# Gate products on tokens and remainders side by side in the dense feed-forwards of a two-block transformer kernel

## The reference

```python
def swiglu(h, w_gate, w_up, w_down):
    return (jax.nn.silu(h @ w_gate) * (h @ w_up)) @ w_down

# first block, layer i (0 and 1)
    h = rms_norm(x, ffn_norm[i]) * (1.0 + sc_f) + sh_f
    x = x + g_f * swiglu(h, ffn_w_gate[i], ffn_w_up[i], ffn_w_down[i])
# second block, layer 0
    h = layer_norm(alpha * h + g2 * swiglu_2(h * (1 + sc2) + sh2, ffn_gate, ffn_up, ffn_down), ln_g, ln_b)
```

## Time and profile before

| | us |
|---|---|
| median of 3 runs (lowest, highest) | 2221.87 (2220.83, 2222.57) |
| profiled execution | 2224.2 |
| its span | 2222.3 |
| TensorE busy | 2176.0 (98%) |
| VectorE busy | 1852.4 (83%) |
| ScalarE busy | 1335.8 (60%) |
| GpSimd busy | 86.2 (4%) |
| ada rows, issue to landing, median | 8.0 |

### The profile page before, as it was taken

How to read it: one execution, slowest core, us unless ns; L and a number is a source line. 1 busy time by engine, 2 the same in 40 slices (tenths; PEclk the granted TensorE clock), 3 DMA queues, 4 the chain that set the end, 5 groups by cost and what they waited for, 6 DMA issues and landing times.

```text
span 2222.3 us, 32055 instructions
## 1 busy us (share of the span) xinstructions
PE 2176.0 (98%) x13109; PEld 1918.6 (86%) x13123; DVE 1852.4 (83%) x2332; ACT 1335.8 (60%) x1508; POOL 86.2 (4%) x140
## 2 busy tenths in 40 slices
PE   6999999999999999999999999999999999999998
PEld 4888999889999979999798888888888888888886
DVE  7867888876998677888896988888888988888897
ACT  3574433665343776434633877777767777777775
POOL 3000111000010000010000000000000000000000
PEclk9999999999999999999999999999999999999999
DMA  9845988625887616885553999999999999999991
GB/s 369 297 186 200 341 325 300 227 77 209 303 298 272 223 39 253 307 332 187 204 201 105 369 348 369 344 370 351 353 366 345 364 346 369 344 364 354 357 363 70
DMA packets 259218, 633.33 MB, mean 285 GB/s; under 512 B 9304, under 2 KB 21625, under 8 KB 258554
## 3 DMA queue, kind: packets, MB, share of 16 engines
q1 hardware_dynamic: 234554, 536.83, 66.4%
q0 software_dynamic: 24512, 94.38, 11.4%
HBM read 630.13 MB, written 1.05 MB: 284 GB/s over the span
## 4 chain that ended last, share of the span: by engine, by line
PE 83%; DVE 11%; DMA 3%; issue 2%; ACT 1%; SPq 0%; POOL 0%; ACTq 0%; DVEq 0%
PE ps L1225 81%; DVE wring_rounded L3019 3%; DMA aring<-in_ada_rows 3%; DVE aring L3046 2%; DVE work L3019 1%; PE ps L2284 1%; PE ps L1421 1%; DVE OT L3043 1%; DVE F L3026 1%; DVE X L3026 0%; DVE F L3019 0%; PE ps L1396 0%; ACT scr_rounded L2349 0%; ACT F_rounded L2349 0%; DVE work_rounded L3019 0%
## 5 line engine op out<-in xcount | busy, mean ns | idle before, releaser
L3019 DVE TENSOR_TENSOR wring_rounded<-wring,scr_rounded 128x2048 fp32r<-128x2048 f32 (+1 forms) x314 | 568.9, 1840 | 76.0 <-ACT scr_rounded L2349 75.9
L2349 ACT ACTIVATE scr_rounded<-wring 128x2048 fp32r<-128x2048 f32 (+1 forms) x314 | 480.0, 1554 | 194.9 <-PE ps L1225 131.4
L1225 PE MATMUL ps<-wring_rounded,OT_rounded 128*128 128x512 f32 (+1 forms) x1184 | 314.8, 390 | 2.7 <-DVE wring_rounded L3019 1.7
L1225 PEld LDWEIGHTS ps<-wring_rounded,OT_rounded 128*128 128x128 f32 x1184 | 220.1, 188 | 47.2 <-DVE wring_rounded L3019 2.3
L3046 DVE CUSTOM_DVE_ANT_0 aring<-aring,F,vec 128x1024 f32<-128x1024 f32 x152 | 187.9, 1283 | 34.2 <-DMA aring<-in_ada_rows 33.5
L3019 DVE TENSOR_TENSOR wring_rounded<-wring,H_rounded 128x2048 fp32r<-128x2048 f32 (+1 forms) x85 | 193.3, 2275 | 25.5 <-ACT H_rounded L2349 25.3
L3019 DVE TENSOR_TENSOR wring_rounded<-wring,aring_rounded 128x2048 fp32r<-128x2048 f32 x84 | 192.4, 2290 | 16.2 <-ACT aring_rounded L2349 16.2
L2349 ACT ACTIVATE H_rounded<-wring 128x2048 fp32r<-128x2048 f32 (+1 forms) x85 | 162.4, 1910 | 61.0 <-issue 39.5
L2349 ACT ACTIVATE aring_rounded<-wring 128x2048 fp32r<-128x2048 f32 x84 | 161.2, 1919 | 58.1 <-PE ps L1225 57.4
L1225 PE MATMUL ps<-V_rounded,wring_rounded 128*128 128x256 f32 x1184 | 177.9, 285 | 4.6 <-DVE wring_rounded L3019 4.6
L1225 PE MATMUL ps<-work_rounded,F_rounded 128*128 128x256 f32 x1056 | 169.8, 283 | 0.0
(11 more groups left out here) (366 smaller groups left out, 3728.2 us busy)
## 6 DMA issues: line engine op xcount, KB each, us to landing
wring<-in_moe_gate SPq DMA_DIRECT2D x56, 2048.0 KB, 8.1
wring<-in_moe_up SPq DMA_DIRECT2D x56, 2048.0 KB, 8.8
wring<-in_moe_down SPq DMA_DIRECT2D x56, 2048.0 KB, 8.2
aring<-in_ada_rows POOLq DMA_DIRECT2D x88, 1024.0 KB, 8.0
wring<-in_ffn_w_gate SPq DMA_DIRECT2D x10, 2048.0 KB, 10.7
wring<-in_ffn_w_up SPq DMA_DIRECT2D x10, 2048.0 KB, 14.5
wring<-in_ffn_w_down SPq DMA_DIRECT2D x10, 2048.0 KB, 10.3
wring<-in_diff_w_in SPq DMA_DIRECT2D x6, 2048.0 KB, 15.7
```

Of the source, the lines that this page charges most:

```text
L1225: return pe.matmul(dst, lhsT, rhs, start=start, stop=stop, **kw)
L2349: return act.activation(dst, src, ACT.Copy, **kw)
L3019: return ve.tensor_tensor(dst, x, y, op)
```

## The change

The remainders and the rounded tokens are put side by side in one tile, `HV`, and a view of it (`Hparts`) gives both as one moving operand of 512 columns. In the gate, the rounded weights are multiplied with this operand, so that one product of 512 columns takes the place of two of 256 with the same weights. The left half of the bank then holds rounded by rounded, the right half rounded weights by remainders of tokens, and the weights' remainders by rounded tokens are added to the right half. Each half m of the gate so needs a bank of its own: banks 0 and 1 in every pair. The up projection is computed as before, in bank 2 or 3, and the sines' jobs move to the up's bank. Pair 0 keeps products of 256 columns, and clears three banks instead of two.

The two halves are added on other engines. ScalarE copies the left half of each of the two banks to SBUF (`ff_main`), VectorE adds the right half to it (`parts_sum`) and frees the bank, and ScalarE takes the Silu in SBUF (`ff_silu`) after the rounding of the next gate's weights; the rounding of the down weights now follows the Silu's wait. The remainder of the gated product is no longer VectorE's; GpSimd subtracts it, and its row loads stand between these subtractions (`feed_forward` on GpSimd). Some semaphores of the mixers are merged, without a change of order.

The diff, without the merged semaphores of the mixers, cut to its core:

```diff
@@ -337,9 +337,10 @@
         X = sb("X", [P, KT, T])
-        H, Hr = sb2("H", [P, KT, T])
+        HV, HVr = sb2("HV", [P, 2, KT * T])
+        H, Hr = (t[:, 1, :].rearrange("p (k t) -> p k t", k=KT) for t in (HV, HVr))
+        V, Vr = HV[:, 0, :], HVr[:, 0, :]
         F, Fr = sb2("F", [P, 24, T])
-        V, Vr = sb2("V", [P, 2048])
         OT, OTr = sb2("OT", [P, KT, T])
@@ -488,16 +490,16 @@
             for n in range(FG):
-                L["gj"].append(J(2 * (n % 2)))
-                L["uj"].append(J(2 * (n % 2) + 1))
+                L["gj"].append([J(0), J(1)])
+                L["uj"].append([J(2 + n % 2)])
                 if f == 2 and n in SIN_GROUPS:
-                    hy_sin.append(J(2 * (n % 2)))
+                    hy_sin.append(J(2 + n % 2))
...
@@ -927,6 +929,7 @@
         Hlower = Hlr.rearrange("p (k t) -> p k t", k=KT)
+        Hparts = HVr[:].rearrange("p s (k t) -> p s k t", k=KT)
 
@@ -1202,7 +1205,29 @@
 
-            for n, c in enumerate(ada1):
+            def feed_forward(f, L):
+
+                rows = [(c, f + 1, 2 * n) for n, c in enumerate(L["a"])]
+                if f == 0:
+                    rows = [(c, 0, 16 + 2 * (EARLY + n)) for n, c in enumerate(ada1[EARLY:])] + rows
+                asked, used = 0, 0
+                for n in range(FG):
+                    late = min(PIECES[f][n], 2) + (len(LATE[n]) if f == 0 and n in LATE else 0)
+                    used += PIECES[f][n] == 3
+                    while asked < min(used + 2, len(rows)):
+                        load_rows(*rows[asked])
+                        asked += 1
+                    pool.wait_ge(ff_hid_upper, FG * f + n + 1)
+                    if n >= 2:
+                        pool.wait_ge(down_used, (FG - 1) * f + n - 1)
+                    pool.tensor_tensor(ff_hidden(n, True), ff_gated(n), ff_hidden(n, False).bitcast(F32),
+                                       ALU.subtract).then_inc(ff_hid_lower, 1)
+                    used += late
+                    while asked < min(used + 2, len(rows)):
+                        load_rows(*rows[asked])
+                        asked += 1
+
+            for n, c in enumerate(ada1[:EARLY]):
                 if n == 8:
@@ -1215,8 +1240,7 @@
                     condition_rows((df_y, ml_y)[f - 1], ((1, 2), (1,))[f - 1])
-                for n, c in enumerate(ffn[f]["a"]):
-                    load_rows(c, f + 1, 2 * n)
+                feed_forward(f, ffn[f])
 
@@ -1463,62 +1487,63 @@
 
...
+                gate, (up,) = L["gj"][n], L["uj"][n]
+                wg, wu = ff_weights(L, n, "g"), ff_weights(L, n, "u")
+                if n == 0:
+                    first_pair(f, gate, up, wg, wu)
+                    return
+                for m, job in enumerate(gate):
+                    job.open(pe)
                     for k in range(KT):
                         if m == 0 and k % 4 == 0:
...
-                        mm(dst, ff_buffer(kind, k // 4)[:, k % 4, m * P:(m + 1) * P], Hupper[:, k, :], k == 0, False)
+                            pe.wait_ge(ff_upper, ff_count(f, n, "g", k // 4))
+                        mm(PS[job.b][:, :], ff_buffer("g", k // 4)[:, k % 4, m * P:(m + 1) * P], Hparts[:, :, k, :], k == 0, False)
                     for k in range(KT):
                         if m == 0 and k % 4 == 0:
...
+                            pe.wait_ge(ff_lower, ff_count(f, n, "g", k // 4))
+                        last = mm(PS[job.b][:, T:2 * T], wg[:, k, m * P:(m + 1) * P], Hupper[:, k, :], False, k == KT - 1)
+                    fill(job, last)
+                up.open(pe)
+                for m in range(2):
+                    dst = PS[up.b][:, m * T:(m + 1) * T]
+                    for q, (rounded, x) in enumerate(((True, Hupper), (False, Hupper), (True, Hlower))):
+                        for k in range(KT):
+                            if m == 0 and k % 4 == 0 and q < 2:
+                                pe.wait_ge(ff_lower if q else ff_upper, ff_count(f, n, "u", k // 4))
+                            w = (ff_buffer("u", k // 4)[:, k % 4] if rounded else wu[:, k])[:, m * P:(m + 1) * P]
+                            last = mm(dst, w, x[:, k, :], q == 0 and k == 0, q == 2 and k == KT - 1)
+                fill(up, last)
+
+            def first_pair(f, gate, up, wg, wu):
+
+                for job in (*gate, up):
+                    job.open(pe)
                     mm(PS[job.b][:, :], zero[:], con[:, 0:2 * P].bitcast(BF16), True, False)
+
+                def places(kind, m):
+                    if kind == "g":
+                        return PS[gate[m].b][:, 0:T], PS[gate[m].b][:, T:2 * T]
+                    return (PS[up.b][:, m * T:(m + 1) * T],) * 2
+
...
                     pe.wait_ge(hi_tile, HI_TILES[FFN_NORM[f]] + k + 1)
-                    for kind, job, w in sides:
+                    for kind, w in (("g", wg), ("u", wu)):
                         if k % 4 == 0:
                             pe.wait_ge(ff_upper, ff_count(f, 0, kind, k // 4))
                             pe.wait_ge(ff_lower, ff_count(f, 0, kind, k // 4))
                         for m in range(2):
+                            main, rest = places(kind, m)
+                            mm(main, ff_buffer(kind, k // 4)[:, k % 4, m * P:(m + 1) * P], Hupper[:, k, :], False, False)
+                            mm(rest, w[:, k, m * P:(m + 1) * P], Hupper[:, k, :], False, False)
+                for kind in "gu":
...
@@ -2495,31 +2520,32 @@
                     gate, up = L["gj"][n], L["uj"][n]
-                    gate.filled(act)
-                    if n == 0:
-                        ff_split(f, L, 1, "g")
                     if n >= 2:
                         act.wait_ge(ff_hid_lower, FG * f + n - 1)
-                    act.activation(ff_gated(n), PS[gate.b][:, :], ACT.Silu).then_inc(gate.bank.free, 1)
-                    if 0 < n < FG - 1:
+                    for m, job in enumerate(gate):
+                        job.filled(act)
+                        copy(ff_gated(n)[:, m * T:(m + 1) * T], PS[job.b][:, 0:T]).then_inc(ff_main, 1)
+                    if n + 1 < FG:
                         ff_split(f, L, n + 1, "g")
+                    gate[1].emptied(act)
+                    act.activation(ff_gated(n), ff_gated(n), ACT.Silu).then_inc(ff_silu, 1)
                     L["d"][n // 2].loaded(act)
                     if n >= 2:
                         act.wait_ge(down_used, (FG - 1) * f + n - 1)
                     copy(down_upper(n), down_weights(L, n, False)).then_inc(down_upper_made, 1)
                     if n in beside:
                         beside[n]()
-                    up.filled(act)
+                    up[0].filled(act)
                     if n + 1 < FG:
                         ff_split(f, L, n + 1, "u")
-                    up.emptied(act)
+                    up[0].emptied(act)
                     copy(ff_hidden(n, False), ff_gated(n)).then_inc(ff_hid_upper, 1)
 
@@ -3345,7 +3371,15 @@
 
+                def parts_sum(n, jobs, dst):
+
+                    for m, job in enumerate(jobs):
+                        ve.wait_ge(ff_main, 2 * (FG * f + n) + m + 1)
+                        main = dst[:, m * T:(m + 1) * T]
+                        tt(main, main, PS[job.b][:, T:2 * T], ALU.add).then_inc(job.bank.free, 1)
+
                 for n in range(FG):
+                    parts_sum(n, L["gj"][n], ff_gated(n))
                     if n + 1 < FG:
@@ -3353,17 +3387,12 @@
                        ALU.subtract).then_inc(down_lower_made, 1)
-                    gate, up = L["gj"][n], L["uj"][n]
-                    gate.emptied(ve)
+                    up, = L["uj"][n]
                     up.filled(ve)
+                    ve.wait_ge(ff_silu, FG * f + n + 1)
                     tt(ff_gated(n), ff_gated(n), PS[up.b][:, :], ALU.mult).then_inc(up.bank.free, 1)
                     if n + 1 < FG:
                         ff_lower_parts(f, L, n + 1, "u")
-                    ve.wait_ge(ff_hid_upper, FG * f + n + 1)
-                    if n >= 2:
-                        ve.wait_ge(down_used, (FG - 1) * f + n - 1)
-                    tt(ff_hidden(n, True), ff_gated(n), ff_hidden(n, False).bitcast(F32),
-                       ALU.subtract).then_inc(ff_hid_lower, 1)
                     if n == 0:
```

More of the change, by code:

```diff
@@ L1490, in hidden_pair @@
-                for side in sides:
-                    side[1].open(pe)
-                if n == 0:
-                    first_pair(f, sides)
-                    return
-                for side in sides:
-                    for m in range(2):
-                        rounded(side, m)
-                        remainder(side, m)
-            def first_pair(f, sides):
-                for _, job, _ in sides:
+                            pe.wait_ge(ff_lower, ff_count(f, n, "g", k // 4))
+                        last = mm(PS[job.b][:, T:2 * T], wg[:, k, m * P:(m + 1) * P], Hupper[:, k, :], False, k == KT - 1)
```

57 lines of the change are left out of this document (20 added, 37 removed).

## The result

The changed kernel takes 2242.93 us (median of 3 runs, 2240.70 to 2243.44) beside 2221.87 before: ratio 1.0091, 95% interval 1.0078 to 1.0105, 21 us slower. The forecast was 2229.2, with a range of 2219.0 to 2236.5, and the time lies above it. The direction was right, the size was not.

A forecast was written before the change was run, and what follows sets the result against it. TensorE, busy 98%, was taken to bound most pairs and VectorE four distances in f = 1. Stage terms 0.6 + 2.95 + 3.75 = +7.3 us on the median 2221.9 gave 2229.2 us, range 2219.0 to 2236.5.

The forecast's parts named there:

- f = 0: First feed-forward stage: start +1.25, five TensorE pairs -1.05, four pairs tied to row transfers +0.4; sum +0.6 us.
- f = 1 and after it: Second feed-forward stage: four VectorE-bound distances lengthen, five TensorE pairs shorten; sum +2.95 us, nothing counted for what follows.
- f = 2 with its start: Third feed-forward stage: late start +3.2, clock dip +1.65, first pairs' hand-over +0.8, nine TensorE pairs -1.9; sum +3.75 us.
- What bounds the kernel: TensorE sets most pairs' pace, 17.28 to 17.07 us (-0.21); VectorE binds four distances in f = 1.
- Bank 2: Start of f = 2: clearing bank 2 waits for VectorE's read of the norm's deviations, so products start 3.2 us later.
- The additions: VectorE's two additions of 128x256 with one operand in PSUM add 0.66 us to each pair.
- GpSimd beside VectorE: GpSimd's 512-column subtraction slows VectorE's remainders and row sums by 0.7 us a pair, between 0 and 1.15.
- the second rival: GpSimd and VectorE lock each other out: +4.5 us, 2233.7, up to 2238 if TensorE's clock drops in f = 1; chance 0.15.
- The Silu's place: Down weights' rounding follows the Silu: VectorE waits 0.34 us in pairs it binds; first down rounding 0.35 later.
- The clock: Start of f = 2: one dip to 1.2 GHz after TensorE idles some 2.65 us, +1.65 us.
- The rivals: Four other outcomes: GpSimd costs VectorE nothing (0.25), full lock (0.15), in between (0.13), VectorE nowhere sets the pace (0.05).

## Why the prediction was wrong

The 0.0091 comes apart by the runs: GpSimd's subtraction 0.0034, the Silu's place 0.0028, bank 2 in f = 2 0.0018, and 0.0011 for the rest, additions less saved products. In us: 7.6, 6.2, 4.0, 2.4. Each of these but bank 2 is a difference of ratios, known to some 0.002, and each holds a share of low clock that differs between executions. By stages the table has +4.05 in f = 0 (forecast 0.6), +8.6 in f = 1 and after it (2.95), and +5.6 in f = 2 with its start (3.75).

- **What bounds the kernel**: right. Where VectorE binds, each of its instructions counts; elsewhere a pair went to 17.11 (forecast 17.07, -0.17 instead of -0.21).
- **Bank 2**: right. 3.09 against 3.2, and 1.2 to 1.5 against 1.65 for the clock, where it falls.
- **The additions**: right, 0.67 a pair: the pair of 18.49 is 17.82 and this.
- **GpSimd beside VectorE**: the step that failed first. I took 0.7 from the row nearest in shape and had 1.15 as an upper end; it is 1.10. That row's VectorE instruction has one wide operand in SBUF and scalars for each row. The Trainium skill (SBUF — State Buffer, Who interferes with whom) has two operands in SBUF as the condition, and these runs agree: with two operands on both sides VectorE's instruction ends 1.08 us after GpSimd's, 165 times out of 165 in five kernels. VectorE's instruction stands until GpSimd's is over, as the second rival had it. A value at this end would have given 2233. The larger miss is where it falls. I counted it as VectorE's time only, and set it against the 0.60 that leaves: net 2.2 us in the sum (ten times 0.7 less eight times 0.60), 7.6 by the runs. It lies on the half of the up remainders for which TensorE stands waiting (1.49 us, in the first pairs too), and in f = 1's end it lengthens a row sum and makes the last down projection wait 0.57.
- **The Silu's place**: the other failed step. Its 0.34 in a bound pair was right (0.32). But I took VectorE's gate remainders as cover in each pair, and the last pair has none (2.50), nor have the first pairs, where VectorE is waiting for everything. I had 0.35 for each first pair, and it was 0.52; at the end of f = 1 with what follows I had nothing, and it was 2.5 us together with GpSimd's subtraction, 0.4 without it.
- **The clock**: I counted one low stretch, at the start of f = 2, and there was a second in f = 2's first pair. Of 18 first pairs with GpSimd's subtraction, in six profiles, six have such a stretch, each after a wait of about 1.5 us; of 24 without it, in eight profiles, none. In the pairs of f = 1 that VectorE bounds, with the same wait, the changed kernel's clock stayed at 1.00. Its other two runs show less low clock over the whole (a mean of 0.995 granted, 0.993 in the profiled one) and take 2243.44 and 2240.70, so the clock isn't the main part.
- **f = 0**: +0.6 against +4.05, of which an unknown part is chance: two executions of the kernel before differ by 3.2 us there, by the landing of rows and up to 1.7 us of clock. With GpSimd's subtraction the long distance was 21.35 to 23.31 in six kernels, without it 18.46 to 21.59 in eight profiles. The distance goes with the clock: 18.46 to 20.30 where that never falls in f = 0's row stretch, 20.97 to 22.81 with 3.4 us of 0.50, 23.18 to 23.31 with 6.8. How much of what the subtraction adds in f = 0 is the lock and how much the loads behind it in GpSimd's queue, no run tells apart.
- **The rivals**: the second, a full lock, was the right one for what GpSimd does to one VectorE instruction, at 0.15, and it had the clock falling after TensorE's waits, though in other pairs than it did. No rival had the last pair.

## What to carry to other kernels

A move to an idle engine is priced by what it does to its neighbours' instructions at the moment at which it must run: look at which instruction the same event releases on the other engine, and who waits for that one. When a wait is hidden by the work of a next iteration, price the first and the last iteration by themselves. A cheaper product is only worth having where its engine sets the pace, and a choice by pair (18 of 33), with the other two parts undone or mended, took a loss of 0.9% to a gain of 0.1%.

## What the runs showed of the hardware

- Beside a GpSimd instruction with two operands in SBUF, a VectorE instruction with two operands there ended 1.08 us after GpSimd's, with 512 columns and with 256, in every one of 165 places. It lost 1.10 and 0.55 us by it. Custom row sums did the same (2.30 instead of 1.28). Beside a GpSimd instruction of one operand it lost 0.42 and ended 0.20 after.
- A VectorE instruction under way held up GpSimd's subtraction of 512 columns: 1.30 us with none, 1.53 with 0.4 us of one left, 1.99 with 0.8 left.
- After an idle stretch of 2.65 us TensorE's clock was 0.50 for 3.4 us in five of seven profiles and stayed at 1.00 in two. In the changed kernel it fell 0.6 us before work began again (876.3 and 876.85), in the kernel before with the wait for bank 2 about 1.2 us after (862.9 and 861.8). A wait of 1.5 us was followed by such a stretch in six first pairs.
